# Attention stage of a decoder block on one core: VectorE normalises a group's result one step later

## The chip, the core and the metric

The kernel runs on one core of one Trainium2 chip. A core has TensorE (PE: matrix products and transposes, results in PSUM), VectorE (DVE), ScalarE (ACT), GpSimd (POOL) and SyncE (SP, which here only starts transfers). The engines run side by side, each through its own list of instructions in order, and wait for each other through semaphores. The metric is the time of one launch on the device in microseconds; lower is better.

## What is computed

A decoder block: a recurrent branch and an attention branch side by side, merged and projected, then a mixture of experts. The change is in the attention, eight heads of 128 dimensions over 1024 tokens, which per head and per block of 128 queries computes

```
s = q[:, lo:hi] @ k[:, :hi]^T * scale
s = s + c[lo:hi, None] - c[None, :hi]          # c: running sum of the log forget gates
s = where(causal, s, -inf)
p = softmax(s)
out = p @ v[:, :hi]
```

## The kernel before

The kernel is a chain of stages (norm, first values, halves, recurrent values, branch 0 out, attention, branch 1 out, projection and routing, experts). Each is a block in which every engine has its own list, and the next stage starts when the engines are through with the block.

In the attention a tile is one block of 128 queries of one head. A pass of the loop (`turns` = 4) does two heads, 16 tiles; tile n of a pass belongs to head n // 8 and to query block 7 - n % 8, so that every head begins with its largest tile (1024 keys) and ends with its smallest (128 keys). Four tiles make a group: the first four tiles of a head (blocks 7 to 4) are its large group, g = 1, with 8 key blocks; the last four are its small group, g = 0, with 4 key blocks.

Precision is kept by splitting: a factor is a high part (rounded) and a low part (the rest), and a product is three products. So a tile passes through these operations:

- scores, PE (lines 1356 to 1368), into the first two PSUM pairs by n % 2;
- bias, mask and row minimum in one operation, DVE (line 1464). The mask for the diagonal block is added to the bias by POOL beforehand (line 1349), after the bias has been loaded (for a head's first tile) or after the tile before has gone through line 1464;
- exponential and row sum, ACT (line 1416); reciprocal of the row sum, DVE (line 1461);
- transposes, PE (`turn`, line 1376), in one or two parts, which take turns on three PSUM banks: a part waits for the low parts of the part three before it (line 1374);
- high parts, ACT (line 1410), and low parts, DVE (`low`, line 1439);
- for each group of four tiles: the value products, PE (`values`, line 1391), and the product with the reciprocals, DVE (`output`, line 1448), which empties the one PSUM bank that holds the result. The value products of the next group wait for it (`o_out`, line 1385).

The reciprocals of a group come to line 1448 by a detour: SP writes them to memory (line 1300), waits until they have landed, and reads them back broadcast over the partitions (line 1303). SP's list for a head is: reciprocals of the large group; store the result of the small group of the head before (line 1295, waits for `output`); load values (line 1222); reciprocals of the small group; load the next bias (line 1218); store the result of the large group. Queries and keys, 2 MB a head, are loaded through ACT's queue (line 1215), after a head's last exponential.

What sets the order is a step number written into each engine's list. In step n PE does scores of tile n, then, if tile n - 8 is the last of its group, that group's value products, and then the transposes of tile n - 4. ACT does the exponential of tile n and the high parts of tile n - 3. DVE does the reciprocal of tile n - 2, line 1464 for tile n, then `output` if tile n - 8 is the last of its group, and then the low parts of tile n - 4. Value products, and `output`, fall into steps 3, 7, 11 and 15 of a pass: in steps 3 and 11 those of a large group, in steps 7 and 15 those of a small one. After the last pass a tail of steps without scores empties the pipeline.

Of the kernel before, what the change touches and what calls it, by code (L numbers as in the profile page):

```python
# [101 lines left out]
class Kernel:  # L102
# [1122 lines left out]
    def attention(self):  # L1225
# [24 lines left out]
        turns, tiles = NH // 2, 2 * NT  # L1250
# [7 lines left out]
        VALUES = 8  # L1258

        def piece(pt, st):  # L1260
            n, kb, m = parts[st]
            qb = block_of(n)
            return pt[qb // 4][:, kb:kb + m, qb % 4 * P:qb % 4 * P + P]

        def back(i, n, by):

            if n - by >= 0:
                return (i, n - by) if n - by < tiles else None
            return None if type(i) is int and i == 0 else (i - 1, n - by + tiles)

        def steps(engine, step):

            for n in range(tiles):
                step(0, n)
            with engine.Fori(1, turns) as i:
                for n in range(tiles):
                    step(i, n)
            for n in range(tiles, tiles + VALUES + 1):
                step(turns - 1, n)

        def later(engine, semaphore, count):

            if type(count) is not int or count > 0:
                engine.wait_ge(semaphore, count)

        with nc.Block() as block:
# [68 lines left out]
            def _(pe):  # L1355
# [14 lines left out]
                def turn(i, n):  # L1370
                    pe.wait_ge(exped, tiles * i + n + 1)
                    for st in of_tile[n]:
                        _, kb, m = parts[st]
                        later(pe, lo, len(parts) * i + st + 1 - TURNED)
                        for j in range(m):
                            mm = pe.transpose(turned(st)[:, j * P:(j + 1) * P],
                                              sb[n % NT][:, (kb + j) * P:(kb + j + 1) * P], k_.ident[:, :])
                        mm.then_inc(t_mm, 1)
# [16 lines left out]
                def step(i, n):  # L1395
# [4 lines left out]
                    if tile := back(i, n, AHEAD):  # L1400
                        turn(*tile)
                steps(pe, step)

            @block.scalar
            def _(act):
                def high(i, n):
                    for st in of_tile[n]:
                        act.wait_ge(t_mm, len(parts) * i + st + 1)
                        later(act, pv_mm, 4 * i + n // 4 - 1)
                        act.activation(piece(pt_h, st), turned(st).rearrange("p (k q) -> p k q", q=P),  # L1410
                                       ACT.Copy).then_inc(hi, 1)

                def exponent(i, n):
                    keys = (block_of(n) + 1) * P
                    act.wait_ge(least, tiles * i + n + 1)
                    act.activation(sb[n % NT][:, 0:keys], sb[n % NT][:, 0:keys], ACT.Exp, scale=-1.0,
                                   bias=small[:, n % 2, 0:1], accum_out=small[:, n % 2, 1:2]).then_inc(exped, 1)

                def step(i, n):
                    if n < tiles:  # L1420
                        exponent(i, n)
                    if n % NT == NT - 1 and n < tiles and (type(i) is not int or i < turns - 1):
                        k_.load_head_qk(act, i + 1, n // NT)
                    if tile := back(i, n, AHEAD - 1):
                        high(*tile)
                for n in range(tiles):
                    step(0, n)
                with act.Fori(1, turns - 1) as i:
                    for n in range(tiles):
                        step(i, n)  # L1430
                for n in range(tiles + VALUES + 1):
                    step(turns - 1, n)

            @block.vector
            def _(dve):
                def low(i, n):
                    for st in of_tile[n]:
                        dve.wait_ge(hi, len(parts) * i + st + 1)
                        dve.tensor_tensor(piece(pt_l, st), turned(st).rearrange("p (k q) -> p k q", q=P),
                                          piece(pt_h, st).bitcast(F32), ALU.subtract).then_inc(lo, 1)  # L1440

                def output(i, group):
                    c, g = group // 2, 1 - group % 2
                    dve.wait_ge(inv_in[g], 16 * (2 * i + c + 1))
                    later(dve, stored[g], 16 * (2 * i + c))
                    dve.wait_ge(pv_mm, 4 * i + group + 1)
                    by_block = lambda v: v.rearrange("d (b p) -> d b p", p=P)
                    dve.tensor_tensor(by_block(o_sb[g][:, :]), by_block(result),
                                      inv_b[g][:, :].rearrange("d (p b) -> d b p", b=4), ALU.mult).then_inc(o_out, 1)

                def step(i, n):
                    before = back(i, n, 2)
                    if before:
                        dve.wait_ge(exped, tiles * before[0] + before[1] + 1)
                    if n < tiles:
                        dve.wait_ge(s_mm, tiles * i + n + 1)
                        dve.wait_ge(masked, tiles * i + n + 1)
                    if before:
                        _, m = before
                        at = block_of(m)  # L1460
                        dve.reciprocal(inv[m // NT][:, at:at + 1], small[:, m % 2, 1:2]).then_inc(inverted, 1)
                    if n < tiles:
                        c, keys = n // NT, (block_of(n) + 1) * P
                        dve.tensor_tensor_reduce(out=sb[n % NT][:, 0:keys], in0=k_.ps[n % 2][:, 0:keys],  # L1464
                                                 in1=bias[c][:, 0:keys], scale=1.0, scalar=-NEG, op0=ALU.add,
                                                 op1=ALU.min, accum_out=small[:, n % 2, 0:1]).then_inc(least, 1)
                    if (tile := back(i, n, VALUES)) and tile[1] % 4 == 3:
                        output(tile[0], tile[1] // 4)
                    if tile := back(i, n, AHEAD):
                        low(*tile)  # L1470
                steps(dve, step)

    def project_route(self):
# [934 lines left out]
```

## Time and profile before

| | us |
|---|---|
| median of 3 runs | 1783.64 (1778.39 to 1786.0) |
| the profiled execution | 1786.07 |
| its span in the trace | 1784.5 |
| busy: PE, DVE, ACT, POOL | 1665.3, 1204.2, 886.6, 135.7 |
| of the span: before the attention, attention, after it | 762, 162, 861 |

The span is the time from the first to the last instruction in the trace; the 1.6 us between it and the execution's time lie around it. Everything below is in microseconds from the span's start. In the timeline rows the columns are: start, duration, engine, line, operation, output and inputs with the shape, and how many instructions are merged in the row; in brackets how long the engine had been idle before it and what released it. A row of several instructions begins with the first. PEld is the load of weights into PE, and an engine's name with a q is its queue of transfers.

### The profile page before, as it was taken

How to read it: one execution, taken by the hardware profiler on the slowest of the kernel's cores; microseconds unless marked ns; L12 is line 12 of the kernel's file. 1: busy time of each engine (PE TensorE's matmuls, PEld its weight loads, DVE VectorE, ACT ScalarE, POOL GpSimd, SP SyncE). 2: the span in 40 equal slices, each digit the busy share in tenths (PEclk: the TensorE clock that was granted, in tenths of full speed). 3: DMA queues.
4: the chain of work that ended last, by engine and by line, in shares of the span. 5: the costliest groups of instructions: out<-in, count | busy, mean ns of one | idle time of the engine just before them, and what ended most of it. 6: DMA issues, size and time to landing. Idle time of an engine off the chain costs nothing. (4 is left out here: it accounts for less than half of the span.)

```text
span 1784.5 us, 22876 instructions
## 1 busy us (share of the span) xinstructions
PE 1665.3 (93%) x8336; PEld 1331.0 (75%) x8336; DVE 1204.2 (67%) x1441; ACT 886.6 (50%) x995; POOL 135.7 (8%) x187
## 2 busy tenths in 40 slices
PE   5999999999999999989989999689999999999990
PEld 5878888888888897877868798566677777777760
DVE  5877776654544653276764434779988888888876
ACT  5333334332555341065642102257777777777762
POOL 1000000000000000021100000100000000000015
PEclk9999999999999999999999999789999999999995
DMA  4335444342323233557863231499999999999977
GB/s 149 100 121 190 152 150 133 95 130 86 104 70 102 83 107 107 200 205 232 234 201 112 100 112 60 159 355 397 391 398 392 399 394 399 392 398 393 397 281 276
DMA packets 181078, 390.58 MB, mean 219 GB/s; under 512 B 15680, under 2 KB 91600, under 8 KB 179984
## 3 DMA queue, kind: packets, MB, share of 16 engines
q1 hardware_dynamic: 166880, 330.62, 51.6%
q0 software_dynamic: 8384, 29.63, 5.3%
q10 hardware_dynamic: 5744, 29.40, 4.4%
q8 instruction: 43, 0.70, 0.2%
q14 instruction: 27, 0.22, 0.0%
HBM read 322.15 MB, written 67.46 MB: 218 GB/s over the span
## 5 line engine op out<-in xcount | busy, mean ns | idle before, releaser
L1886 DVE TENSOR_TENSOR e_l<-e_raw,e_h 128x2048 fp32r<-128x2048 f32 x192 | 439.1, 2290 | 65.3 <-ACT e_h L1880 65.0
L1880 ACT ACTIVATE e_h<-e_raw 128x2048 fp32r<-128x2048 f32 x192 | 367.9, 1917 | 85.2 <-PE ps L1915 50.1
L1902 PE MATMUL ps<-e_h,e_xth 128*96 128x512 f32 x512 | 205.2, 401 | 6.3 <-DVE e_l L1886 3.0
L1902 PE MATMUL ps<-e_h,e_xtl 128*96 128x512 f32 x512 | 202.6, 396 | 0.0
L1902 PE MATMUL ps<-e_l,e_xth 128*96 128x512 f32 x512 | 201.9, 394 | 0.0
L213 PE MATMUL ps<-uh,w_h 128*128 128x512 f32 x512 | 162.4, 393 | 10.6 <-DVE ul L1177 5.3
L213 PE MATMUL ps<-uh,w_l 128*128 128x512 f32 x512 | 161.2, 391 | 0.0
L213 PE MATMUL ps<-ul,w_h 128*128 128x512 f32 x512 | 161.2, 391 | 0.0
L213 PEld LDWEIGHTS ps<-uh,w_h 128*128 128x128 f32 x512 | 96.5, 189 | 32.4 <-issue 10.8
L1902 PEld LDWEIGHTS ps<-e_h,e_xth 128*96 128x96 f32 x512 | 83.0, 162 | 46.6 <-issue 7.4
L213 PEld LDWEIGHTS ps<-ul,w_h 128*128 128x128 f32 x512 | 97.0, 189 | 20.4
L213 PEld LDWEIGHTS ps<-uh,w_l 128*128 128x128 f32 x512 | 96.7, 189 | 20.2
L1902 PEld LDWEIGHTS ps<-e_h,e_xtl 128*96 128x96 f32 x512 | 83.1, 162 | 36.2
L795 DVE TENSOR_TENSOR wn_stl<-wn_stl,ps 128x512 f32<-128x512 f32 x112 | 76.8, 686 | 46.1 <-PE ps L741 40.3
L1902 PEld LDWEIGHTS ps<-e_l,e_xth 128*96 128x96 f32 x512 | 83.4, 163 | 32.1
L1915 PE MATMUL ps<-e_h,e_hth 128*96 128x512 f32 x256 | 82.5, 403 | 2.1 <-DVE e_htl L2036 2.1
L193 ACT ACTIVATE w_h<-w_raw 128x2048 fp32r<-128x2048 f32 x22 | 42.0, 1908 | 79.6 <-DMA w_raw<-w_lru_out 42.6
L1915 PE MATMUL ps<-e_l,e_hth 128*96 128x512 f32 x256 | 80.5, 395 | 0.0
L1915 PE MATMUL ps<-e_h,e_htl 128*96 128x512 f32 x256 | 80.2, 394 | 0.0
L225 PE MATMUL ps<-w_h,uh 128*128 128x256 f32 x256 | 74.3, 290 | 4.4 <-DVE w_l L197 2.4
L1967 POOL DMA_INDIRECT e_xg<-xn_d,slots_i x30 | 41.4, 1379 | 474.7 <-PE ps L1978 474.7
L1367 PE MATMUL ps<-at_qk 128*128 128x512 f32 (+3 forms) x288 | 70.1, 372 | 7.4 <-DVE at_small L1464 5.4
(685 smaller groups left out, 3404.8 us busy)
## 6 DMA issues: line engine op xcount, KB each, us to landing
e_raw<-w_exp_gate SPq DMA_DIRECT2D x64, 1024.0 KB, 20.1
e_raw<-w_exp_up SPq DMA_DIRECT2D x64, 1024.0 KB, 20.1
e_raw<-w_exp_down SPq DMA_DIRECT2D x64, 1024.0 KB, 19.4
wn_raw<-w_in SPq DMA_DIRECT2D x32, 512.0 KB, 5.2
w_raw<-w_in SPq DMA_DIRECT2D x12, 1024.0 KB, 5.3
at_qk<-qk_d ACTq DMA_DIRECT2D x6, 2048.0 KB, 10.2
y_d<-e_y ACTq DMA_DIRECT2D x32, 384.0 KB, 6.4
y_d<-zeros POOLq DMA_DIRECT2D x22, 384.0 KB
```

Of the source, the lines that this page charges most:

```text
L193: act.activation(self.w_h[s][:, :, :], self.w_raw[s][:, :, :], ACT.Copy).then_inc(self.w_hi[s], 1)
L213: mm = pe.matmul(ps[:, h * HALF:(h + 1) * HALF], w[:, k, :], u[:, k, h * HALF:(h + 1) * HALF], start=first, stop=last)
L225: mm = pe.matmul(ps, u[:, k, rows], w[s][:, k, :], start=first, stop=last)
L795: dve.tensor_tensor(out, part, bank(n, name), ALU.add).then_inc(added, 1)
L1367: mm = pe.matmul(k_.ps[n % 2][:, at:end], q, qk[c][:, part, at:end], start=first, stop=last)
L1880: act.activation(self.e_h[m % SPLIT][:, :, :], self.e_raw[slot][:, :, :], ACT.Copy).then_inc(self.e_hi[m % SPLIT], 1)
L1886: dve.tensor_tensor(self.e_l[slot][:, :, :], self.e_raw[slot][:, :, :], self.e_h[m % SPLIT][:, :, :].bitcast(F32), ALU.subtract).then_inc( ...
L1902: mm = pe.matmul(ps, x[:, k, :], w[:, k, :], start=first and first_piece, stop=last and last_piece)
L1915: mm = pe.matmul(ps[:, c * HALF:(c + 1) * HALF], x[:, at, :], w[:, 2 * k + c, :], start=first, stop=last)
L1967: pool.indirect_dma_start(out=xg[b][:, :], out_offset=None, in_=k_.xn_d, in_offset=bass.IndirectOffsetOnAxis(ap=slots, axis=0)).then_inc(g ...
```

## The change

`output` is called in the step after the one in which PE makes the group's value products, at the same place within the step: behind line 1464 and ahead of the low parts. So it moves behind the low parts of tile n - 4 of its old step, and behind the reciprocal and line 1464 of the next step. DVE and ACT also go through one more step at the end, in which nothing is due. The other engines' lists are the same.

```diff
@@ steps(), DVE and PE @@
-            for n in range(tiles, tiles + VALUES + 1):
+            for n in range(tiles, tiles + VALUES + 2):
                 step(turns - 1, n)
@@ scalar @@
-                for n in range(tiles + VALUES + 1):
+                for n in range(tiles + VALUES + 2):
                     step(turns - 1, n)
@@ vector, step(i, n) @@
                         dve.tensor_tensor_reduce(...)        # line 1464, tile n
-                    if (tile := back(i, n, VALUES)) and tile[1] % 4 == 3:
+                    if (tile := back(i, n, VALUES + 1)) and tile[1] % 4 == 3:
                         output(tile[0], tile[1] // 4)
                     if tile := back(i, n, AHEAD):
                         low(*tile)
```

On VectorE, after a large group's value products, the list before (steps 11 and 12: `at_o` is the group's result, `at_ptl` low parts, `at_s` line 1464's output with the minimum in `at_small`):

```order
L1448 TENSOR_TENSOR at_o_6908<-ps,at_invb_6926 128x512 [waits na_prm_mm,na_powered]
L1439 TENSOR_TENSOR at_ptl_6912<-ps,at_pth_6910 128x128 [waits na_x7]
L1461 RECIPROCAL at_inv_6924<-at_small 128x1 [waits na_x1,na_x2,na_x4]
L1464 ISA at_s_6918,at_small<-ps,at_bias_6533 128x512
L1464 ISA at_small 128x1
L1439 TENSOR_TENSOR at_ptl_6913<-ps,at_pth_6911 128x4x128 [waits na_x7] x2
```

The same place after the change:

```order
L1439 TENSOR_TENSOR at_ptl_6912<-ps,at_pth_6910 128x128 [waits na_x7]
L1461 RECIPROCAL at_inv_6924<-at_small 128x1 [waits na_x1,na_x2,na_x4]
L1464 ISA at_s_6918,at_small<-ps,at_bias_6533 128x512
L1464 ISA at_small 128x1
L1448 TENSOR_TENSOR at_o_6908<-ps,at_invb_6926 128x512 [waits na_prm_mm,na_powered]
L1439 TENSOR_TENSOR at_ptl_6913<-ps,at_pth_6911 128x4x128 [waits na_x7] x2
```

The result's product now stands between the 512-key tile and the two low parts of the 1024-key tile.

After a small group's value products, on VectorE, where one pass ends and the next begins, before:

```order
L1464 ISA at_s_6921,at_small<-ps,at_bias_6533 128x128
L1464 ISA at_small 128x1
L1448 TENSOR_TENSOR at_o_6907<-ps,at_invb_6925 128x512 [waits na_prm_mm,na_averaged]
L1439 TENSOR_TENSOR at_ptl_6913<-ps,at_pth_6911 128x4x128 [waits na_x7]
L1439 TENSOR_TENSOR at_ptl_6913<-ps,at_pth_6911 128x128 [waits na_x7]
L1275 UNCONDITIONAL_BRANCH
L1275 ISA
L1456 ISA [waits na_x4]
L1461 RECIPROCAL at_inv_6924<-at_small 128x1 [waits na_x1,na_x2]
L1464 ISA at_s_6914,at_small<-ps,at_bias_6532 128x1024
L1464 ISA at_small 128x1
L1438 ISA
```

And after the change:

```order
L1439 TENSOR_TENSOR at_ptl_6913<-ps,at_pth_6911 128x4x128 [waits na_x7]
L1439 TENSOR_TENSOR at_ptl_6913<-ps,at_pth_6911 128x128 [waits na_x7]
L1275 UNCONDITIONAL_BRANCH
L1275 ISA
L1456 ISA [waits na_x4]
L1461 RECIPROCAL at_inv_6924<-at_small 128x1 [waits na_x1,na_x2]
L1464 ISA at_s_6914,at_small<-ps,at_bias_6532 128x1024
L1464 ISA at_small 128x1
L1444 ISA
L1284 REGISTER_ALU [waits na_averaged]
L1446 ISA [waits o_stored0]
L1448 TENSOR_TENSOR at_o_6907<-ps,at_invb_6925 128x512 [waits na_prm_mm]
```

The result's product, with its waits for the reciprocals (`na_averaged`), for the store of the result before it (`o_stored`) and for the value products (`na_prm_mm`), now stands behind the next head's 1024-key tile and ahead of the low parts of the 512-key tile.

## Rows read from the trace of the kernel before

**Rows 1.** Busy time by stretch: duration, busy PE, PEld, DVE, ACT, POOL, clock, DMA share, GB/s.

```profile
762.00:924.00 162.00, 147.13 (x864) 125.81 (x864) 113.33 (x304) 92.94 (x225) 29.81 (x66) 0.98 0.71 213
```

**Rows 2.** Waits in 762 to 926: who waited for whom, total us, times, longest.

```profile
POOL at_bias L1349 <- DMA at_bias<-bias_d: 17.8, 5, 6.4
DVE at_o L1448 <- DMA at_invb<-inv_d: 7.1, 4, 2.3
```

**Rows 3.** Timeline of DVE after a large group's value products.

```profile
847.55 1.12 DVE L1448 TENSOR_TENSOR at_o<-ps,at_invb 128x512 f32<-128x512 f32 x1 [2.75 <-PE ps L1391]
848.57 0.29 DVE L1439 TENSOR_TENSOR at_ptl<-ps,at_pth 128x128 fp32r<-128x128 f32 x1
...
848.84 0.68 DVE L1464 CUSTOM_DVE_ANT_0 at_s<-ps,at_bias 128x512 f32<-128x512 f32 x1
...
849.53 1.29 DVE L1439 TENSOR_TENSOR at_ptl<-ps,at_pth 128x512 fp32r<-128x512 f32 x2
```

**Rows 4.** Timeline of ACT and PE in the same stretch.

```profile
847.40 0.94 PE L1367 MATMUL ps<-at_qk 128*128 128x512 f32 x3
...
847.68 0.28 ACT L1410 ACTIVATE at_pth<-ps 128x128 fp32r<-128x128 f32 x1 [3.37 <-PE ps L1376]
...
852.01 0.44 PE L1376 MATMUL ps<-ident,at_s 128*128 128x128 f32 x2 [0.39 <-DVE at_ptl L1439]
```

**Rows 5.** Timeline of DVE and PE, first tiles of the second and third head.

```profile
778.64 1.22 DVE L1464 CUSTOM_DVE_ANT_0 at_s<-ps,at_bias 128x1024 f32<-128x1024 f32 x1
...
796.82 1.21 DVE L1464 CUSTOM_DVE_ANT_0 at_s<-ps,at_bias 128x1024 f32<-128x1024 f32 x1
...
798.76 1.08 DVE L1464 CUSTOM_DVE_ANT_0 at_s<-ps,at_bias 128x896 f32<-128x896 f32 x1
...
799.91 1.25 PE L1367 MATMUL ps<-at_qk 128*128 128x512 f32 x6
```

**Rows 6.** Where the bias comes late: POOL, PE, PE's clock, last head's DVE.

```profile
818.11 0.45 POOL L1349 TENSOR_TENSOR at_bias<-at_bias,at_mask 128x128 f32<-128x128 f32 x1 [6.44 <-DMA at_bias<-bias_d]
...
875.49 0.46 POOL L1349 TENSOR_TENSOR at_bias<-at_bias,at_mask 128x128 f32<-128x128 f32 x1 [2.95 <-DMA at_bias<-bias_d]
...
820.02 1.33 PE L1367 MATMUL ps<-at_qk 128*128 128x512 f32 x6 [3.11 <-DVE at_small L1464]
...
822.00:824.00 2.00, 2.00 (x7) 1.71 (x8) 1.63 (x5) 1.73 (x4) 0.78 (x2) 0.50 0.86 295
...
895.52 1.22 DVE L1464 CUSTOM_DVE_ANT_0 at_s<-ps,at_bias 128x1024 f32<-128x1024 f32 x1
```

**Rows 7.** Queues of ACT and SP.

```profile
795.39 0.36 ACTq L1215 DMA_DIRECT2D at_qk<-qk_d  x1
...
796.33 7.18 SPq L1222 DMA_DIRECT2D at_v<-v_d  x2
...
810.20 0.33 SPq L1303 DMA_DIRECT2D at_invb<-inv_d  x1
...
855.59 0.34 ACTq L1215 DMA_DIRECT2D at_qk<-qk_d  x1
...
861.54 1.44 SPq L1222 DMA_DIRECT2D at_v<-v_d  x2
...
869.89 0.33 SPq L1303 DMA_DIRECT2D at_invb<-inv_d  x1
```

**Rows 8.** The stage's last steps: DVE, ACT and PE.

```profile
911.61 1.09 DVE L1448 TENSOR_TENSOR at_o<-ps,at_invb 128x512 f32<-128x512 f32 x1 [0.67 <-PE ps L1391]
...
914.03 0.48 PE L1391 MATMUL ps<-at_pth,at_v 128*128 128x512 f32 x1
...
919.00 1.05 DVE L1448 TENSOR_TENSOR at_o<-ps,at_invb 128x512 f32<-128x512 f32 x1 [3.50 <-PE ps L1391]
...
919.03 0.28 ACT L1410 ACTIVATE at_pth<-ps 128x128 fp32r<-128x128 f32 x1 [4.18 <-PE ps L1376]
...
920.31 0.49 PE L1391 MATMUL ps<-at_pth,at_v 128*128 128x512 f32 x1 [1.31 <-DVE at_ptl L1439]
```

## The prediction, made before the change was run

> **What bounds the kernel now.** I read the stage's share first. The attention takes 162 us of the span of 1784.5; PE is busy 147.1 of them and DVE 113.3 [rows 1]. The change touches nothing outside it, so all that it can move are these 162 us, and what it moves there is handed on whole to the stages behind. Then the waits of the stage by total, then DVE's, PE's and POOL's timelines around the sixteen results (line 1448), then the queues.
>
> The reader is to see three things. First, PE is nearly always at work in the stage, but not on its own pace: after a large group's value products it runs into DVE. DVE works without a gap from the result at 847.55 to the low parts at 849.53 and on, and PE's transposes at 852.01 had to wait 0.39 us for them [rows 3, 4]. Second, where nothing is late, one head follows another at 796.82 - 778.64 = 18.18 us (start of the 1024-key tile in line 1464) [rows 5]. Third, later heads are slower than that: from 778.64 to 895.52 are six heads in 116.88 us, 19.48 each [rows 5, 6]. The 1.3 us a head between the two are the bias. POOL waited five times for its transfer, 17.8 us in all [rows 2], once until 818.11, for which PE stood still 3.11 us, and ran at half clock (0.50) afterwards [rows 6]. So two chains run at nearly the same pace: DVE with PE at 18.2 us a head, and the transfers at about 19.5.
>
> **The change, part by part.** It adds no work. Sixteen results of about 1.1 us each (1.12, 1.09 and 1.05 in [rows 3, 8]) change their place on DVE. The empty step at the end costs nothing: no operation is issued in it. The question is what each result stands in front of, before and after.
>
> After a large group (step 4 of a head), before: value products end, result at 847.55, low parts of the 128-key tile at 848.57, line 1464 at 848.84, low parts of the 1024-key tile at 849.53 [rows 3]. The high parts of the 128-key tile were there at 847.68 + 0.28 = 847.96 [rows 4], so the result held those low parts back by 0.6 us. That is all there is to gain: without it DVE would be through with them at 848.27, but line 1464 needs the scores, which PE has at 847.40 + 0.94 = 848.34 [rows 4], so it starts near 848.40 instead of 848.84, 0.44 sooner. Behind it now stands the result, 1.05 us with the overlap of one operation into the next (848.57 - 847.55 = 1.02). The low parts of the 1024-key tile start at 849.53 - 0.44 + 1.03 = 850.1, 0.6 later. DVE has no gap behind that and PE's transposes wait for the low parts at 852.01, with nothing in hand [rows 3, 4]. So term A is +0.6 us, once a head, and it reaches the small group's value products. Bounds: 0, if the start of line 1464 were the only thing that mattered, to 1.0, the result's whole time.
>
> After a small group (step 8, on the next head's first tile): before, the result stands ahead of the low parts of the 640-key tile, whose high parts come at about the same time as it ends, so that it costs nothing there. Then line 1464 at 796.82, low parts, line 1464 again at 798.76 until 799.84, and PE's scores at 799.91, which wait for this second one [rows 5]. After the change the result stands between the two, and the 1024-key tile cannot start sooner, because it waits for its scores. So the second starts at 799.8 and PE's scores at 800.9: term B is +1.0 us a head. Behind it DVE has idle time again (2.75 us ahead of a large group's result [rows 3]) but PE has not, so nothing of it comes back. Bounds: 0.2, if PE had another 0.8 in hand, to 1.1.
>
> A and B together make the undisturbed pace 18.18 + 1.6 = 19.78 us a head. That is the first result of the working: the engines' own pace becomes slower than the transfers' pace of about 19.5, and so most of the waits for the bias go away, and their cost with them. This is where I choose, for it depends on what the transfers do when the engines come later.
>
> Queries and keys are asked for at 795.39 and 855.59, and SP has the small group's reciprocals in memory and goes on at 810.20 and 869.89, 14.8 and 14.3 later [rows 7], although the loads of values began 0.9 us after the one request and 6.0 after the other (796.33, 861.54 [rows 7]). So this part of the chain ends at a fixed time after the request for queries and keys, and a start of the values' load up to 5 us later is covered by it. That matters because SP stores a small group's result ahead of the load of values, and now the result comes about 3 us later: behind a step's rest and a line 1464 of 1.2 us. The Trainium skill, page DMA: Bandwidth & Descriptors, section Issuing engines are not separate DMA queues, says that transfers started from different engines run on the same 16 DMA engines and interleave. By that rule the later store costs nothing, as the equal 14.8 and 14.3 say too; if the queues were independent, SP's 3 us would all be added to the bias, the rival below.
>
> From the request to the bias in place is 875.49 - 855.59 = 19.9 us [rows 6, 7], and line 1464 can start 0.6 behind it (mask on POOL 0.46). Where nothing is late the request comes 796.82 - 795.39 = 1.4 us ahead of the next head's first tile [rows 5, 7], and A and B move both alike, so line 1464 could start 20.5 - 1.4 = 19.1 us behind that tile, and the next is due at 19.78. It fits with 0.7 to spare. One transfer may be longer: that of 818.11 came 22.7 us after its request at 795.39 [rows 6, 7], because the next queries and keys were asked for soon after the bias; with heads 1.6 us longer these lie further apart. I allow 0.7 us for all waits that are left.
>
> Sum, from the start of the second head's first tile. Before: 116.88 to the last head's. After: 18.18 + 0.6 for the first head (no result stands behind its first tile) and 5 x 19.78 = 98.90, that is 117.68; +0.8, and 0.7 for waits, +1.5. In the last head B once, +1.0, and A once, +0.6. Then the end: the result at 911.61 now follows the low parts and the reciprocal and ends near 914.6, and the last large group's value products, which began at 914.03, wait for it: +0.6 [rows 8]. The result at 919.00 follows the low parts whose high parts end at 919.03 + 0.28, and begins at 919.6: the last value products start near 920.65 instead of 920.31, and SP stores and then loads the next stage's inputs behind the same result, +0.5 [rows 8]. In all 1.5 + 1.0 + 0.6 + 0.6 + 0.5 = **+4.2 us**.
>
> The clock is part of this. PE's halt of 3.11 us was followed by a stretch at a granted 0.50, the lower of its two levels (1.2 GHz) [rows 6]. The 2 us of that row hold 1 us of work at the full clock, so 1 us or more of this head is the clock's; it is contained in the 116.88 and not in the 19.78. The Trainium skill, TensorE: Matmul & The Clock Gate, section HAM oscillation, tells the same: a wait for a DMA that is long enough sends the array back to the slow clock, and the work behind it starts slow. By that rule the waits that the change adds, each under 1.1 us, cost no clock, and the halt that goes away gives about 1 us back; the sum would be that much more if the halt stayed.
>
> **Rivals.**
> - The transfers keep their distance (slower). If the bias comes later by what SP is held up, or by what the engines are, the old waits stay and the new terms are added in full: A for seven heads, 4.2, B for six, 6.0, and the end, 1.1: +11.3 us. For it: SP does store the result ahead of the loads; one bias needed 22.7 us. Against it: the fixed 14.3 to 14.8. It decides as soon as the way from the request to the tile takes more than 19.78 + 1.4 = 21.2 us.
> - The wait for the reciprocals goes away (faster). Four results waited 7.1 us for their reciprocals [rows 2] with low parts and the next head's first tile behind them; one step later they are there. All of it and the clock back would be -8.6 us. Against it: the tile behind such a result needs the bias as well, which came late at 818.11 and, with the mask, about when DVE was through at 875.49 [rows 6], and its scores. So it gives 0.1 or 0.2 us a head at the most, and only as long as the bias isn't later.
> - It is a wash. PE's wait of 0.39 us for DVE shows how tight both are [rows 4]; where PE's transposes have a little in hand in step 9, B shrinks, and pace stays at the transfers' 19.5: 0 to +1.5 us.
>
> **How the numbers follow.** The profiled execution took 1786.07, its sum would be 1790.3; it lies 2.4 above the median of the runs, to which the change is added: 1783.64 + 4.2 = 1787.8 us. A measurement of this kernel can tell about 0.5%, 8.9 us, from no change. Chances: the forecast (+2 to +7 us) 0.60; the wash 0.22; the transfers keep their distance 0.14; the reciprocals 0.04. The forecast and the wash lie within 0.5%. The slower rival's 11.3 lies over it, most of its chance with it: 0.12 slower. The fast one's 8.6 is just short of it: 0.03 faster. The range goes from 1780, half of the fast rival with a median that can itself lie 2 us elsewhere, to 1796, the slower rival's 1794.9 and a little: A at its upper bound and B at its upper bound would be 0.4 and 0.1 a head more, which with the pace set by the engines is +3 on the forecast, inside the range.
>
> **What the changed kernel's profile would show.** The results start right behind a 512-key or a 1024-key tile of line 1464 and wait for nothing: neither value products nor reciprocals (before 12 and 4 waits, now at most the last one or two). PE's waits for low parts after a large group grow from 0.39 to about 1 us, and its scores in step 11 wait about 1 us for line 1464. The first tiles of heads lie 19.6 to 20 us apart; POOL's waits for the bias no longer hold up DVE, and the halt of 3.11 with the half clock is gone. The stage takes about 166 us instead of 162, all others the same. I would be wrong in B if PE did not wait in step 11, in the transfers if DVE still waited for POOL's mask by 1 us or more at several heads, and altogether if the stage took under 161 or over 171 us.

## The result and the profile after

| | before | after |
|---|---|---|
| median | 1782.66 us (20 runs) | 1787.97 us (20 runs) |
| ratio, after to before | | 1.0029, 95% interval 1.002 to 1.0038 |
| profiled execution, its span | 1786.07, 1784.5 | 1786.95, 1785.2 |
| first tile of the second head to that of the last | 116.88 | 117.16 |
| from there to the last result | 27.06 | 29.73 |

The kernel became 5.3 us slower (3.6 to 6.8 by the interval); +4.2 and 1787.8 had been forecast. That 1787.8 and 1787.97 lie so close is luck: the forecast was added to 1783.64, the median of three runs, and that of twenty is 1.0 lower. The two profiled executions lie only 0.9 apart (for the one after, 1790.3 had been forecast), so half of what follows is about that too.

The timeline of DVE after the change, behind a large group's value products; it answers to [rows 3]:

```profile
847.93 0.29 DVE L1439 TENSOR_TENSOR at_ptl<-ps,at_pth 128x128 fp32r<-128x128 f32 x1 [3.21 <-ACT at_pth L1410]
...
848.40 0.67 DVE L1464 CUSTOM_DVE_ANT_0 at_s<-ps,at_bias 128x512 f32<-128x512 f32 x1
...
848.99 1.08 DVE L1448 TENSOR_TENSOR at_o<-ps,at_invb 128x512 f32<-128x512 f32 x1
849.99 1.28 DVE L1439 TENSOR_TENSOR at_ptl<-ps,at_pth 128x512 fp32r<-128x512 f32 x2
```

The idle time in front of the result, 2.75 us before, now stands in front of the small low parts, and the result stands 1.0 us wide between line 1464 and the low parts of the 1024-key tile. From the small low parts to these it is 849.99 - 847.93 = 2.06 us; before it was 849.53 - 848.57 = 0.96.

The same behind a small group's, DVE and PE, second and third head (answers to [rows 5]):

```profile
779.22 1.22 DVE L1464 CUSTOM_DVE_ANT_0 at_s<-ps,at_bias 128x1024 f32<-128x1024 f32 x1
...
798.05 1.20 DVE L1464 CUSTOM_DVE_ANT_0 at_s<-ps,at_bias 128x1024 f32<-128x1024 f32 x1
...
799.18 1.12 DVE L1448 TENSOR_TENSOR at_o<-ps,at_invb 128x512 f32<-128x512 f32 x1
...
800.90 1.06 DVE L1464 CUSTOM_DVE_ANT_0 at_s<-ps,at_bias 128x896 f32<-128x896 f32 x1
...
802.02 1.25 PE L1367 MATMUL ps<-at_qk 128*128 128x512 f32 x6 [0.83 <-DVE at_small L1464]
```

From the first line 1464 to the second it is 2.85 us instead of 1.94, and PE's scores of step 3, which had begun at 799.91 with no wait for DVE, wait 0.83 us. (The third head begins a pass; in the second head of a pass the same place is step 11.) That wait is there in all six heads behind a small result (0.82 to 1.09).

Four of the waits of the stage after the change, 755 to 935:

```profile
POOL at_bias L1349 <- DMA at_bias<-bias_d: 12.7, 5, 3.0
DVE at_inv L1461 <- POOL at_bias L1349: 5.7, 18, 0.7
DVE at_o L1448 <- PE ps L1391: 2.4, 1, 2.4
PE ps L1391 <- DVE at_o L1448: 2.2, 2, 1.7
```

The waits of results for reciprocals (7.1 us, [rows 2]) are gone, and those for value products have shrunk to the last one. PE waits twice for a result: these are the two waits at the stage's end. POOL's longest wait for a bias is 3.0 instead of 6.4, and DVE's longest for POOL 0.7; the halt of 3.11 [rows 6] is gone.

### The profile page after: what moved, and what is told of

Its sections match the earlier page's. It is cut to its first block and busy times, and to the rows that moved or that the text cites. A ratio compares the mean times of both kernels' runs of the same rounds, so it can differ in the third digit from the quotient of the medians.

```text
span 1785.2 us, 22879 instructions
## 1 busy us (share of the span) xinstructions
PE 1659.4 (93%) x8336; PEld 1326.0 (74%) x8336; DVE 1203.1 (67%) x1441; ACT 888.9 (50%) x995; POOL 136.8 (8%) x187
## 5 line engine op out<-in xcount | busy, mean ns | idle before, releaser
L213 PEld LDWEIGHTS ps<-uh,w_l 128*128 128x128 f32 x512 | 96.8, 189 | 20.4
L1439 DVE TENSOR_TENSOR at_ptl<-ps,at_pth 128x512 fp32r<-128x512 f32 (+1 forms) x96 | 50.3, 554 | 38.7 <-ACT at_pth L1410 38.7
## 6 DMA issues: line engine op xcount, KB each, us to landing
e_raw<-w_exp_up SPq DMA_DIRECT2D x64, 1024.0 KB, 19.4
```

Of the source, the lines that this page charges most:

```text
L213: mm = pe.matmul(ps[:, h * HALF:(h + 1) * HALF], w[:, k, :], u[:, k, h * HALF:(h + 1) * HALF], start=first, stop=last)
```

## Experiments

All times are beside those of the kernel before, measured on the same chip with them. "Six heads" is the start of the second head's 1024-key tile in line 1464 to that of the last head.

**One half alone.** The small groups' results one step later:

```diff
-                    if (tile := back(i, n, VALUES + 1)) and tile[1] % 4 == 3:
+                    if (tile := back(i, n, VALUES)) and tile[1] % 8 == 3:
+                        output(tile[0], tile[1] // 4)
+                    if (tile := back(i, n, VALUES + 1)) and tile[1] % 8 == 7:
```

> Only the results of the small groups come one step later; those of the large groups stay where they were. Theory (two terms, and a pace of the transfers that hides them): the term B (0.8 us a head, as the changed kernel's first tiles give it) makes the undisturbed pace 18.18 + 0.8 = 19.0 us a head, still below the 19.5 at which the bias comes, so the heads from the second first tile to the last stay at about 116.9 us, with PE's halt of some 3 us at the fourth head shortened; what is added is B once in the last head and 0.6 at the end: +1.4, 1784 us. PE waits about 0.8 us for line 1464 in steps 3 and 11, and not more than before for the low parts of the 1024-key tile. Rival (each term is paid in full in every head): 6 x 0.8 + 0.6 = +5.4, 1788 us.

And the large groups' (the two numbers the other way round):

> Only the results of the large groups come one step later. Theory: A (0.65 us a head) makes the pace 18.8, below 19.5, so the heads stay at about 117 us; A once in the last head, 0.4 for the last value products, 0.5 behind the last large result: +1.5, 1784 us. The two halves then give less than the whole change's +5.3 together. Rival (paid in full): 7 x 0.65 + 0.9 = +5.5, 1788 us.

Each was measured at 1.0012 times the kernel before, interval 1.0002 to 1.0022, so +2.1 us (0.4 to 3.9) each; medians 1783.98 and 1782.53 beside 1780.56. "Paid in full", +5.4 and +5.5, lies outside; +1.4 and +1.5 inside. Six heads took 114.85 and 114.43 us, not the 116.9 and 117 that were expected: these figures came from the first profile of the kernel before, which was a slow one (see below). Beside its second profile (114.36, and 27.09 to the last result) the small groups' half is 2.1 us longer over both parts (28.69 for the last), the large groups' half 1.1 (28.08), and the whole change 5.4. In the first variant, PE waited as foreseen:

```profile
801.49 1.25 PE L1367 MATMUL ps<-at_qk 128*128 128x512 f32 x6 [0.84 <-DVE at_small L1464]
```

In the second, the second and third head are 18.83 us apart, and the later ones that no late bias held up 18.73 to 18.75:

```profile
797.00 1.21 DVE L1464 CUSTOM_DVE_ANT_0 at_s<-ps,at_bias 128x1024 f32<-128x1024 f32 x1
...
815.75 1.20 DVE L1464 CUSTOM_DVE_ANT_0 at_s<-ps,at_bias 128x1024 f32<-128x1024 f32 x1
```

That gives the terms by measurement: A = 18.75 - 18.18 = 0.57 us a head, and with the changed kernel's 817.66 - 798.05 = 19.61, B = 19.61 - 18.75 = 0.86. The rows of the small result itself say about the same: 2.85 - 1.94 = 0.91 from one line 1464 to the next.

**The late bias taken away.** SP's list for a head in another order, once with the old places of the results and once with the new:

```diff
                     inverses(i, c, 1)
+                    if not last:
+                        sp.wait_ge(least, tiles * i + NT * (c + 1))
+                        k_.load_head_bias(sp, i + 1, c)
                     if not first:
                         store(j, d, 0)
-                        if not last or d == 1:
-                            load_v(j + 1, d)
                     inverses(i, c, 0)
-                    if not last: ... load_head_bias
+                    if not first and (not last or d == 1):
+                        load_v(j + 1, d)
                     store(i, c, 1)
```

> The results as in the kernel before, but SP loads the next bias ahead of the small group's store and reciprocals, and the values behind the reciprocals, so that no first tile waits for its bias. Theory: the pace falls from 19.5 to the undisturbed 18.2 us a head, 6 x 1.3 = -7.8 us, less up to 1 us where a result still waits for its reciprocals: 1775 to 1776 us, and no half clock in the stage. Rival (the transfers are bound by their sheer amount, not by SP's order): the 2 MB of queries and keys and the values still take their time, pace 19.0 to 19.5: 0 to -2 us.

> The same order of SP's transfers with both results one step later, as in the changed kernel. Theory: the changed kernel's pace of 19.6 is VectorE's and TensorE's own, so the earlier bias gives almost nothing (0 to -1 us against the changed kernel: 1787 us), and the distance between this kernel and the one with the same transfers and the old results is the full price, A 0.65 x 7 + B 0.8 x 6 + 1.5 at the end = 10.8 us. Rival (the results cost nothing by themselves, what was lost was lost through SP, whose store and loads wait for the result): no distance between the two, within 2 us.

With the new places: 1.0034 (1.0023 to 1.0045), six heads in 117.00 us, as with the old transfers (117.16). No wait for a bias was left, and nothing was won by it. So the changed kernel's pace is that of its own engines, as the theory had it. With the old places: 0.9992 (0.9982 to 1.0001), six heads in 112.37. That is -1.4 us, not clear of no change, where -7.8 less 1 had been expected; it lies in the rival's 0 to -2, and the pace of 18.7 lies between the two. The distance between the two is 1786.89 - 1779.35 = 7.5 us, not 10.8 and not under 2: the results' places cost by themselves, but the old ones didn't reach 18.2. The cause is in the DVE timeline of the old places:

```profile
825.62 1.09 DVE L1448 TENSOR_TENSOR at_o<-ps,at_invb 128x512 f32<-128x512 f32 x1 [3.65 <-DMA at_invb<-inv_d]
...
844.06 1.10 DVE L1448 TENSOR_TENSOR at_o<-ps,at_invb 128x512 f32<-128x512 f32 x1 [3.07 <-DMA at_invb<-inv_d]
```

Large groups' results, which had never waited for reciprocals in the first profile, now did, four times (15.5 us with one small group's). SP read them back when the next 2 MB of queries and keys were under way: asked for at 814.59, read-back issued at 816.66, landed 8.7 us later, 10.8 behind the request. In the kernel before it was no better: asked for at 855.59, read-back issued at 860.69, landed 5.0 later, 10.1 behind the request. But there the late bias held the first tile until 2.1 us behind the request (857.68), here it follows after 1.1 (815.72), and the result, due about 9 us behind the tile, comes to wait. So a wait that the late bias had hidden came out; it was not removed. My expectation of 1 us for it was the miss.

**The small result two steps later.** The large groups' line is that of the kernel before:

```diff
-                    if (tile := back(i, n, VALUES)) and tile[1] % 8 == 7:
+                    if (tile := back(i, n, VALUES + (1 if n >= tiles else 2))) and tile[1] % 8 == 7:
```

> The large groups' results where they were before; the small groups' results two steps later than before (one step in the tail), that is behind line 1464 of the 896-key tile and so behind what TensorE's scores in steps 3 and 11 wait for. Theory (what B costs is the place ahead of that line 1464, not the lateness): B vanishes, the scores of steps 3 and 11 wait no more than 0.3 us, no result waits for its reciprocals; second to last first tile at or a little under the kernel before, 0.6 us at the end: 0 to +1 us against the kernel before, so about 1 to 2 us faster than the variant with one step. Rival (a result costs its time wherever it is put late): as the variant with one step or slower, +2 us or more.

Measured 1.0003 (0.9989 to 1.0017), medians 1783.74 beside 1782.69. The timeline of DVE:

```profile
798.72 1.08 DVE L1464 CUSTOM_DVE_ANT_0 at_s<-ps,at_bias 128x896 f32<-128x896 f32 x1
799.73 0.08 DVE L1464 DVE_READ_ACCUMULATOR2_ANT at_small<- 128x1 f32 x1
799.73 1.09 DVE L1448 TENSOR_TENSOR at_o<-ps,at_invb 128x512 f32<-128x512 f32 x1
```

The tile begins at 1.94 us behind the first one again (798.72 - 796.78), and the result follows it. PE's scores in steps 3 and 11 wait 0.28 us at most. So B's wait is gone, and it is the place ahead of that line 1464 that costs, not the lateness. In the length of the heads this can't be seen here: the bias was late at every later head (POOL waited 19.4 us for it), and six heads took 115.08, no less than the 114.85 with one step. It can be seen in the last variant of the next section, where from 796.78 to 814.99 a head with such a small result took 18.21 us, as undisturbed heads of the kernel before do. The times can't tell this variant from the one with one step (1.0012), since the intervals overlap.

**Values loaded last**, at the end of SP's list for a head (behind `store(i, c, 1)`), the bias where it was:

> The results as in the kernel before; SP loads a head's values at the end of its list for a head, so that the small group's reciprocals and the bias don't queue behind them, and the large group's reciprocals aren't delayed either. Theory: neither the bias nor, at a large group, the reciprocals are waited for; pace 18.2 to 18.5 us a head against 18.7 of the variant with the early bias, so 1 to 3 us less than that one and 2 to 4 us less than the kernel before. Rival (the amount of the transfers sets it): as the early bias, -1 us.

> Both: small results two steps later, values loaded last. Theory: no wait for reciprocals, none for the bias, none for the result: pace 18.2, six heads in 109.2 us, 0.6 at the end; 1 us less than the same transfers with the old results if reciprocals are late there, else equal. 3 to 5 us less than the kernel before.

With the old results 0.9986 (0.9974 to 0.9998), -2.5 us, but by its profile not for the reason given: six heads took 113.56, more than the early bias's 112.37. Four of the six stood at 18.2 us, but in the two others a result waited 3.65 and 5.44 us for its reciprocals; the write of the latter, issued at 866.42, took 12.7 us to land. Behind that wait PE stood still 1.86 and soon after 0.55 us, and its clock fell to 0.50 (886 to 888), so the 21.67 us of this head are in part the clock's. With the small results two steps later as well it was **0.9972 (0.9959 to 0.9985)**, 1778.44 beside 1782.69: faster than the kernel before by about 5 us (2.1 to 7.3), and so by about 10 than the changed one, though no run has these two side by side. Its interval overlaps that of the variant with the old results, so the times don't show what the later small result adds to it. Six heads took 110.90 us instead of the expected 109.2, since two large results still waited for their reciprocals:

```profile
824.53 1.12 DVE L1448 TENSOR_TENSOR at_o<-ps,at_invb 128x512 f32<-128x512 f32 x1 [2.57 <-DMA at_invb<-inv_d]
...
862.32 1.09 DVE L1448 TENSOR_TENSOR at_o<-ps,at_invb 128x512 f32<-128x512 f32 x1 [3.45 <-DMA at_invb<-inv_d]
```

**The profiles themselves, again.** Both kernels unchanged, one more profile of the changed one and two of the one before:

> The kernel before, once more, for a second profile of it. In the first one the fourth head's bias came late (818.11) and TensorE halted 3.11 us, and that execution lay 3.4 us above the median of 20 runs, while the profile of the changed kernel lay 1.0 below its own. Theory: the halt was that execution's own; now the six heads from the second to the last first tile take 114 to 115.5 us instead of 116.88, with no wait for a bias over 1.5 us on VectorE. Rival (the halt belongs to the kernel): 116.5 to 117.5 again.

> The changed kernel once more, for a second profile. Theory (its pace is set by VectorE and TensorE): the six heads take 117.0 to 117.4 us again, and the last first tile to the last result 29.7. Rival (its 117.16 was as much an accident as the 116.88 of the kernel before): off by 1 us or more.

> The kernel before, a third profile. Theory (its pace is set by the transfers, and varies with them; the fourth head's bias is always late, the half clock behind it is not always there): six heads in 114 to 115.5 us, the fourth head 20.5 to 22 us, PE halting 2 to 3 us before it. Rival: 116.9 as in the first profile.

| | six heads | last first tile to last result | third to fourth head's first tile |
|---|---|---|---|
| before, first profile | 116.88 | 27.06 | 21.92 |
| before, second | 114.36 | 27.09 | 21.16 |
| before, third | 113.88 | 27.02 | 20.48 |
| after, first | 117.16 | 29.73 | 19.61 |
| after, second | 117.16 | 30.44 | 19.61 |

The changed kernel's six heads repeat to 0.01 us, those of the one before don't, as a pace set by engines on one side and by transfers on the other lets one expect. The last part of the changed kernel came out 0.7 longer than I wrote; its last result waited 3.06 us for the value products instead of 2.39. That is the clock: both profiles have the same wait of PE for the result ahead of these products (1.74 us), but only in the second did the products slow down behind it (granted 0.51 in 925 to 927, against 1.00 in 924 to 926 of the first). The same product in the first and in the second profile:

```profile
925.29 0.28 PE L1391 MATMUL ps<-at_ptl,at_v 128*128 128x256 f32 x1
```

```profile
925.50 0.41 PE L1391 MATMUL ps<-at_ptl,at_v 128*128 128x256 f32 x1
```

The variant with the early bias and the new places had it too (0.52 in 924 to 926, last result waiting 2.92). The halt at the fourth head belongs to the kernel before (2.32 us in the second profile, 1.71 in the third), against what I expected of the second. In the third profile six heads, fourth head and halt all lay a little under what I expected. The half clock behind the halt does not belong to the kernel. Busy time and PE's clock (the value behind POOL's) in 820 to 824, first, second and third profile of the kernel before:

```profile
820.00:824.00 4.00, 3.71 (x15) 3.05 (x16) 3.59 (x9) 3.53 (x7) 1.38 (x3) 0.71 0.92 332
```

```profile
820.00:824.00 4.00, 3.71 (x21) 2.98 (x20) 3.52 (x10) 3.43 (x8) 0.93 (x2) 1.00 0.95 383
```

```profile
820.00:824.00 4.00, 3.71 (x20) 2.99 (x19) 3.51 (x10) 3.02 (x8) 0.92 (x2) 1.00 0.94 378
```

## Why the prediction was right, and where two errors met

- *The bound.* Right. DVE and PE at 18.2 us a head against transfers at 19 and more; taking the late bias away shortened the six heads of the one (112.37) and not of the other (117.00). By the times alone the first is not clear of no change.
- *A, +0.6 a head.* Measured 0.57. The mechanism is the one foreseen, the small low parts start 0.6 earlier in relation to the value products and the result costs more behind them. PE's wait of 0.39 for the low parts stayed, and one of 0.6 to 0.7 came ahead of it in every head (before the change the rows show 0.19 there, at one head only).
- *B, +1.0 a head.* Mechanism right, size a little high: 0.86 by the heads, 0.91 by the rows, and PE waits 0.83.
- *Pace 19.78.* Measured 19.61. (A + B = 1.43 is no second check of it, since B was taken from this pace.) The first of the six heads, for which 18.78 was forecast, took 18.83.
- *Waits left, 0.7.* 0.3: only one head (19.92) stands out. The way from the request for queries and keys to the bias in place was foreseen as 19.9 us, at times more; it took 19.5 to 20.4, and the small group's reciprocals were read back 14.1 to 14.8 behind the request. In the first profile of the kernel before that last figure had one exception which the prediction passed over: 813.89 to 830.24, 16.4 us.
- *The end, +1.0, +0.6, +0.6 and +0.5, together +2.7.* The stretch from the last first tile to the last result grew by 29.73 - 27.06 = 2.7. The two waits of value products for a result are there: 2.2 us in two waits, 0.51 and 1.74; the second stands where PE had waited 1.31 us for low parts before, so it adds 0.4.
- *The baseline.* This is what failed. The sum counted from 116.88, and that execution was 2.5 to 3.0 us slower in the same stretch than the two later profiles. The head behind the halt is the largest part of that: 19.78 us, and 18.27 and 18.28 in the others. The prediction put the difference between 19.48 and 18.18 down to the bias alone, but in this head it was mostly the half clock. It noticed the half clock and counted 1 us of it as something the change would give back. A usual execution has nothing to give back. The sum against the second profile is 117.16 - 114.36 = 2.8 and 29.73 - 27.09 = 2.6, together 5.4, where the first two profiles give 0.28 and 2.67, together 2.95. The medians show 5.3; with the changed kernel's second profile it would be 6.2; 5.4 and 6.2 both lie in 3.6 to 6.8. By its own working the sum should have been 118.4 for the six heads, 1.2 more than measured; that error and the baseline's 2.5 had opposite signs, and 4.2 lies as near to 5.3 as it does for that reason.
- *The clock.* That the added waits cost no clock was right for those inside the heads (granted 1.00 around them), but not at the end: one of the added waits was 1.74 us and not under 1.1, and in two of three executions with both results later the half clock stood behind it and cost 0.5 to 0.7 us. Nor does the length of a halt tell when the clock falls: 3.11 us and 1.86 (with 0.55 behind it) had the half clock behind them, 2.32 and 1.71 at the place of the 3.11 had not, and 1.74 had it or not. By the Trainium skill, TensorE: Matmul & The Clock Gate, section HAM oscillation, a long enough wait for a DMA brings the slow clock. The halt of 3.11 us behind a late bias agrees with that; the other rows here do not follow the length.
- *The rivals.* The transfers did not keep their distance: the store behind the result, 4.4 us later in the third head (800.33 instead of 795.96, 0.6 of it from ahead of the stage), did not delay the bias, which came at 816.95 instead of 818.11. The reciprocals' waits went away, and nothing that they gave is to be seen; of the -8.6 us of this rival the prediction's rows support 8.1 (7.1 and 1). It was not a wash.

That the two profiled spans differ by 0.7 us only has a part behind the attention as well. In one stretch there the clock of the kernel before fell for a moment and that of the changed one didn't:

```profile
1000.00:1025.00 25.00, 21.74 (x97) 18.43 (x96) 10.32 (x8) 5.94 (x4) 1.42 (x11) 0.89 0.26 88
```

```profile
1004.00:1029.00 25.00, 21.74 (x109) 18.27 (x108) 10.87 (x8) 5.80 (x5) 1.43 (x11) 1.00 0.25 86
```

The changed kernel stood 4.95 us behind at the next stage's first product on DVE (947.43 against 942.48) and 1.0 at the experts' first (1166.3 against 1165.3). The other profiles go the same way: from that product on DVE to the experts' first low parts (line 1886) are 212.0, 210.9 and 209.5 us in the three profiles of the kernel before, 208.0 and 209.3 in the two of the changed one. So what the attention lost was not handed on whole in these executions, as the prediction had supposed, and that its sum and the medians agree to 0.1 us is more than the profiles can bear. What the rest of that is was not tried.

## What to carry to other kernels

An operation that waits should be moved not to where it no longer waits but to where nobody waits for what stands behind it: here the wait in front of the result was idle time anyway, one step later stood the operation on which TensorE's scores hang, and one step later again there was room (which by itself gave no time that could be measured, as long as the bias was late). When a chain of transfers and a chain of engines run at nearly the same pace, the price of a change is what it adds beyond the slower one, so halves of a change need not add up to the whole. The profiles show that here (2.1 and 1.1 us against 5.4); the times (2.1 and 2.1 against 5.3) are too uncertain to show it alone. And if the profiled execution lies 3 us above the median, look for what it has that a usual one lacks before anything in it is booked as a gain.

## What the hardware showed that I had not expected

How long the 2 KB of reciprocals take to land in memory, and with them SP's list, varied with what else was in flight. In the variant with the early bias and the old results SP read back at 827.48 what it had begun to write at 818.18, 9.3 us later, while 2 MB of queries and keys, asked for at 814.59, and a bias were on their way; it read back at 793.16 what it had begun at 791.73, 1.4 us later, with nothing of the kind under way. 2 KB behind 2 MB can take longer than any single operation on VectorE in this stage (1.2 us at most).

PE's clock did not follow its waits closely either. With the same 1.74 us of wait at the same place, in two profiles of the same changed kernel, the products behind it ran at the full clock in one and from 925 on at half in the other.
